# GpSimd makes the second low piece of each half slot of weights, with the residual between them

## The reference

```python
def swiglu(h, w_in, w_out):
    a, u = jnp.split(h @ w_in, 2, axis=-1)
    return (jax.nn.silu(a) * u) @ w_out

def post_norm_residual(x, y, gate, res_w, g, b):
    return layer_norm(DN_ALPHA * x + res_w * (1.0 + gate[:, None, :]) * y, g, b)
...
    mod = c_act @ ada_w[i] + ada_b[i]
    sh0, sc0, g0, sh1, sc1, g1, sh2, sc2, g2 = jnp.split(mod, 9, axis=-1)
```

## Time and profile before

| | |
|---|---|
| median of 3 runs | 4571.94 us (4563.4 to 4573.9) |
| the profiled execution | 4562.87 us, its span 4561.1 us |
| TensorE busy | 3806.3 us (83%) |
| VectorE busy | 3120.1 us (68%) |
| ScalarE busy | 1788.1 us (39%) |
| GpSimd busy | 55.1 us (1%) |
| granted TensorE clock, mean | 0.892 |

### The profile page before, as it was taken

The page is one execution under the profiler, slowest core; times in us unless marked ns, Lnnn a source line. Parts: engine busy times, 40 slices in busy tenths (PEclk is TensorE's granted clock), DMA queues, the critical chain, the costliest instruction groups (busy, mean ns, idle before and its releaser), DMA issues. The chain is left out here.

```text
span 4561.1 us, 65970 instructions
## 1 busy us (share of the span) xinstructions
PE 3806.3 (83%) x26030; PEld 3441.1 (75%) x26030; DVE 3120.1 (68%) x6168; ACT 1788.1 (39%) x3446; POOL 55.1 (1%) x32
## 2 busy tenths in 40 slices
PE   5998899987897752699979987725999799999698
PEld 4986698986797652599879975625998699898587
DVE  6776577765655658866676654488666877687655
ACT  2443444443443230344444442312444444444243
POOL 0000000010000000000000000000000000000000
PEclk9999899997798676699999997765999999999799
DMA  7755475752354121155425542210555366486244
GB/s 295 263 228 196 155 267 215 266 210 102 120 185 157 56 78 43 47 186 191 169 102 185 189 159 96 74 56 29 185 191 188 116 231 234 167 300 245 111 153 148
DMA packets 118965, 751.35 MB, mean 165 GB/s; under 512 B 13184, under 2 KB 13216, under 8 KB 43008
## 3 DMA queue, kind: packets, MB, share of 16 engines
q1 hardware_dynamic: 117648, 742.97, 44.6%
q10 hardware_dynamic: 688, 3.11, 0.2%
q0 software_dynamic: 320, 1.05, 0.1%
HBM read 744.98 MB, written 1.05 MB: 164 GB/s over the span
## 5 line engine op out<-in xcount | busy, mean ns | idle before, releaser
L748 DVE TENSOR_TENSOR weights_low<-weight_ring,weights_high 128x512 fp32r<-128x512 f32 x2248 | 1467.1, 697 | 542.6 <-ACT weights_high L735 529.4
L735 ACT ACTIVATE weights_high<-weight_ring 128x512 fp32r<-128x512 f32 x2248 | 1293.4, 625 | 1069.8 <-PE bank L159 977.6
L159 PE MATMUL bank<-h_high,weights_high 128*128 128x256 f32 x4800 | 1372.0, 286 | 86.2 <-DVE weights_low L748 86.2
L159 PE MATMUL bank<-h_low,weights_high 128*128 128x256 f32 x4800 | 1370.7, 286 | 0.0
L159 PE MATMUL bank<-h_high,weights_low 128*128 128x256 f32 x4800 | 1370.2, 285 | 0.0
L159 PEld LDWEIGHTS bank<-h_high,weights_high 128*128 128x128 f32 x4800 | 933.0, 194 | 105.4 <-issue 88.0
L159 PEld LDWEIGHTS bank<-h_low,weights_high 128*128 128x128 f32 x4800 | 933.1, 194 | 14.4
L159 PEld LDWEIGHTS bank<-h_high,weights_low 128*128 128x128 f32 x4800 | 932.5, 194 | 0.0
L159 PE MATMUL acc<-weights_high,hidden_high 128*128 128x512 f32 x1552 | 609.0, 392 | 3.1 <-DVE weights_low L748 3.1
L159 PE MATMUL acc<-weights_low,hidden_high 128*128 128x512 f32 x1552 | 608.4, 392 | 0.0
L159 PE MATMUL acc<-weights_high,hidden_low 128*128 128x512 f32 x1552 | 603.7, 389 | 0.0
(11 more groups left out here) (254 smaller groups left out, 3386.1 us busy)
## 6 DMA issues: line engine op xcount, KB each, us to landing
weight_ring<-stream SPq DMA_DIRECT2D x582, 1024.0 KB, 4.8
h_tok<-slots SPq DMA_DIRECT2D x96, 512.0 KB, 5.7
h_feat<-slots SPq DMA_DIRECT2D x90, 512.0 KB, 5.8
work<-slots SPq DMA_DIRECT2D x30, 512.0 KB, 7.8
mod_sums<-biases SPq DMA_DIRECT2D x8, 1536.0 KB, 8.2
h_feat<-rows SPq DMA_DIRECT2D x8, 512.0 KB, 4.1
work<-biases SPq DMA_DIRECT2D x1, 1536.0 KB, 9.5
x_tok<-x ACTq DMA_DIRECT2D x1, 1024.0 KB, 11.4
```

What stands on the lines that cost most here:

```text
L159: ins = self.nc.tensor.matmul(out, lhs, rhs, start=start, stop=stop)
L735: act.activation(k.w_hi[:, b, q * self.QUARTER:(q + 1) * self.QUARTER], self.raw(g, q), ACT.Copy).then_inc(k.highs_ready, 1)
L748: ins = dve.tensor_tensor(k.w_lo[:, b, w], self.raw(g, q), k.w_hi[:, b, w].bitcast(F32), ALU.subtract)
```

## The change

The low piece q = 1 of every half is now made by GpSimd, and q = 0 by VectorE as before; each tells TensorE by a semaphore of its own, and TensorE waits for both. `SplitWeights` gets a `gpsimd` method, which replaces `Stage.gpsimd` there: for each half the low piece, and behind those of halves 2, 4, 6 and 8 one of the four operations of the residual. The waits inside the residual (for the rows, and between the multiplications and the additions) stay. `ToTokensAndCouples.gpsimd` still calls its parent's method first, which is now the loop over four halves, and then issues the copies.

```diff
--- before.py
+++ after.py
@@ -106,6 +106,7 @@
         self.slot_landed = [ctx.enter_context(nc.semaphore(f"slot_landed{i}")) for i in range(RING)]
         self.highs_ready = ctx.enter_context(nc.semaphore("highs_ready"))
         self.lows_ready = ctx.enter_context(nc.semaphore("lows_ready"))
+        self.lows_by_pool = ctx.enter_context(nc.semaphore("lows_by_pool"))
         self.halves_used = ctx.enter_context(nc.semaphore("halves_used"))
         self.slots_used = ctx.enter_context(nc.semaphore("slots_used"))
         self.couples_made = ctx.enter_context(nc.semaphore("couples_made"))
@@ -202,8 +203,7 @@
         pass
 
     def gpsimd(self, pool):
-        if self.residual is not None:
-            self.residual.run(pool)
+        pass
 
     def sum_step(self, dve, g):
         for slot in self.macs[g]:
@@ -300,16 +300,20 @@
         for i, place in enumerate(self.places):
             sp.dma_start(place, rows[2 * self.number + i]).then_inc(k.rows_landed, 16)
 
-    def run(self, pool):
-        k = self.k
-        pool.wait_ge(k.rows_landed, 32 * (self.number + 1))
-        for t in range(TT):
+    def part(self, pool, i):
+        k, t = self.k, i % TT
+        if i == 0:
+            pool.wait_ge(k.rows_landed, 32 * (self.number + 1))
+        if i < TT:
             ins = pool.tensor_tensor(k.x[:, t, :], k.h_tok[:, t, :], self.places[0], ALU.mult)
-        ins.then_inc(k.pool_step, 1)
-        pool.wait_ge(k.pool_step, k.step("pool"))
-        for t in range(TT):
+        else:
+            if i == TT:
+                pool.wait_ge(k.pool_step, k.step("pool"))
             ins = pool.tensor_tensor(k.x[:, t, :], k.x[:, t, :], self.places[1], ALU.add)
-        ins.then_inc(k.residual_made, 1)
+        if i == TT - 1:
+            ins.then_inc(k.pool_step, 1)
+        elif i == 2 * TT - 1:
+            ins.then_inc(k.residual_made, 1)
 
 
 
@@ -708,6 +712,7 @@
         for g in range(self.n):
             b = (self.base + g) % DEEP
             pe.wait_ge(k.lows_ready, self.base + g + 1)
+            pe.wait_ge(k.lows_by_pool, self.base + g + 1)
             if g % 2 == 1:
                 k.slots_through()
             self.products(pe, g, k.w_hi[:, b, :], k.w_lo[:, b, :])
@@ -737,17 +742,25 @@
             if g >= 2:
                 self.scalar_after(act, g - 2)
 
+    def low(self, eng, g, q, ready):
+        k = self.k
+        b = (self.base + g) % DEEP
+        w = slice(q * self.QUARTER, (q + 1) * self.QUARTER)
+        eng.wait_ge(k.highs_ready, 2 * (self.base + g) + q + 1)
+        eng.tensor_tensor(k.w_lo[:, b, w], self.raw(g, q), k.w_hi[:, b, w].bitcast(F32), ALU.subtract).then_inc(
+            ready, 1)
+
+    def gpsimd(self, pool):
+        for g in range(self.n):
+            self.low(pool, g, 1, self.k.lows_by_pool)
+            if self.residual is not None and g in (2, 4, 6, 8):
+                self.residual.part(pool, g // 2 - 1)
+
     def vector(self, dve):
         k = self.k
         for g in range(self.n + 2):
-            b = (self.base + g) % DEEP
             if g < self.n:
-                for q in range(2):
-                    w = slice(q * self.QUARTER, (q + 1) * self.QUARTER)
-                    dve.wait_ge(k.highs_ready, 2 * (self.base + g) + q + 1)
-                    ins = dve.tensor_tensor(k.w_lo[:, b, w], self.raw(g, q), k.w_hi[:, b, w].bitcast(F32),
-                                            ALU.subtract)
-                ins.then_inc(k.lows_ready, 1)
+                self.low(dve, g, 0, k.lows_ready)
             if g >= 2:
                 self.vector_after(dve, g - 2)
             self.sum_step(dve, g)
```

## The result

| | before | after |
|---|---|---|
| median | 4568.06 us (4563.4 to 4573.9, 4 runs) | 4610.69 us (4605.55 to 4619.61, 4 runs) |
| span of the profiled execution | 4561.1 us | 4603.8 us |
| TensorE busy | 3806.3 us | 3809.5 us |
| VectorE busy | 3120.1 us | 3034.9 us |
| GpSimd busy | 55.1 us | 1595.3 us |

The account below looks back on a forecast made before the run. TensorE was taken as the bound, with the moved VectorE work nearly all off its path. Terms 15.6 + 17 + 6 + 6.4 + 3 - 4.9 - 1.4 = +41.7 us gave 4614 us, range 4580 to 4662.

Parts of the forecast that it names:

- Starts: At the starts of 26 stages, TensorE begins 0.6 us later because GpSimd makes the second low: +15.6 us.
- The wait behind the residual: VectorE's sum waits for a slot held until the residual's last piece: 8.5 us in two feature stages, 3.0 in two feed-forward.
- Half clock: TensorE gets half its clock behind the residual stalls: 2.2 us per 8.5 us stall, 1.0 per 3 us stall, +6.4 us.
- Gained: Seven short TensorE stalls in the first halves of the stages with a Residual go: -4.9 us.
- Projected: In NSA's "projected" stage, copies behind GpSimd's lows come later and half the 2.72 us stall goes: -1.4 us (+3 if late).
- The dense feed-forward stage: Third part's first feed-forward stage, where VectorE is busiest and the shared port is about full: +3 us (0 to 6).
- Steady stretches: In the peer layers the port needs 2.48 of TensorE's 2.81 us per half: 0; added wait at most 34 us.
- GpSimd's price: One 512-wide low piece on GpSimd was taken to cost 1.25 us, between ends of 1.19 and 2.38.
- Rival B: The SBUF port becomes the bound because a GpSimd low takes 1.45 us or more: 4665 us; chance 0.13.
- Rival D: Stalls compound: late slots keep VectorE late at the next sums and half clock returns, +30, 4644 us; chance 0.14.
- Rival C: Not slower: the sums' slots land before TensorE needs half 7, no stalls there, 4569 us; chance 0.08.

Follow-up runs that it names:

- the pieces alone: Kernel before, but GpSimd does the residual in four pieces after the highs of halves 2, 4, 6, 8; VectorE makes both lows: 4583.33 us, ratio 1.0037.
- the lows alone: Kernel before, but GpSimd makes the second low piece in the 21 stages without a Residual; the other five unchanged: 4579.89 us, ratio 1.0031.

## Why the prediction was right, point by point

The forecast was 4614 us, +42; measured 4610.69, +43. The mechanism of the three large terms, the starts, the wait behind the residual and the half clock behind it, is the one that was forecast, and the runs above bear it out. That the totals agree to 1 us is luck: the terms miss by up to 5 us in both directions, and the measured difference is itself known to some 11 us. The terms, by the traces of the two kernels:

- **Starts**, forecast 0.6 x 26 = 15.6. Counted from ScalarE's first high, TensorE's first product is 0.52 to 0.54 later in all 26, 13.8 us (in six stages TensorE's idle time before it changed by another amount, 0.18 to 2.24 us, as the work before it ended earlier or later); taking them back gave 12 us. The size was a little high since I added the whole of VectorE's first low before GpSimd could begin.
- **The wait behind the residual**, forecast 8.5 twice and 3.0 twice. Measured 7.50, 7.68, 2.48 and 2.63: 20.3 for 23. The term that was too long is the landing, 3.2 us (302.44 to 305.65) where I took 4.1.
- **Half clock**, forecast 6.4. Behind the four stalls, in this order, 24, 27, 16 and 17 products ran at half clock (1.2 GHz), in 5.25, 5.93, 3.51 and 3.53 us, where at full clock one starts every 0.12 us: 10.1 us for these 84, so it cost 8.1. I had given the 3 us stalls 1.0 each; they cost 1.6 and 1.5.
- **Gained**: of the seven stalls of 4.9 us four small ones of 0.42 to 0.47 remain, 1.7 us.
- **"Projected"**, forecast -1.4: this term had the wrong sign. The stall of 2.72 us is gone whole; in "the pieces alone" that stage has it again, at 3.11 us, and in "the lows alone" not. But the copies that now stand behind the four lows end later, and with them the stage. GpSimd's drain at the stage's end (line 180, 181 after) ends 0.2 us after the last copy has landed, in both traces, and all engines wait for it there (the rows below). From the stage's first product to the additions of `Compress` it takes 1041.51 - 1020.52 = 20.99 us before and 1075.04 - 1050.53 = 24.51 after, the later start left out: +3.5 us. "+3 if the copies are late" was the nearer end of the forecast.
- **The dense feed-forward stage**, forecast +3: three stalls of 0.47, 0.47 and 0.74 us, 1.7.
- **Steady stretches**, forecast nothing: the peer stages keep 5.62 us for two halves, and the added wait costs 0 of the 34 us that were its upper bound.

13.8 + 20.3 + 8.1 + 1.7 - 4.9 + 3.5 + 1.7 = +44.2 us, against 42.7 between the two spans. The difference of 1.5 us is within what one execution differs from another: the four runs of the changed kernel lie 14 us apart.

The end of "projected", before and after: GpSimd's drains in the stretch (ns: least/median/most, then the first and last start), and TensorE's first product of the next stage:

```profile
L180 POOLq DRAIN  x2: 41/7706/15371, 1019.9 to 1037.0; - x2
...
1037.02 3.21 PE L159 MATMUL bank<-weight_ring,h_feat 128*128 128x48 f32 x27 [0.72 <-POOLq L180]
...
L181 POOLq DRAIN  x2: 41/5382/10722, 1056.5 to 1067.3; - x2
...
1067.26 7.06 PE L160 MATMUL bank<-weight_ring,h_feat 128*128 128x48 f32 x32 [4.14 <-DVEq L181]
...
1075.04 4.29 DVE L1715 TENSOR_TENSOR work<-work 128x120 f32<-128x120 f32 x16
```

Before, the long drain begins at 1019.9 and lasts 15.37 us, to 1035.2; the last part of the copies landed at 1035.01, ahead of the end of TensorE's last product at 1036.30. After, it begins at 1056.5 and lasts 10.72 us, to 1067.2, where the copies had landed at 1066.99 and TensorE had ended at 1063.12; TensorE starts at 1067.26 after 4.14 idle (the row names VectorE's queue; the drain that came last is GpSimd's). Then it runs the next 32 products at half clock, in 7.06 us; before they took 3.77 at full clock. The gap is 3.20 to 4.31 us in each of the six single-low versions in which GpSimd makes lows in this stage, the changed kernel among them, and 0.72 in the four in which it does not, the kernel before among them. How much of the half clock comes with it differs from run to run, so over all ten traces the stage is 1.6 us longer on average rather than 3.5. No run took this wait away alone, and issuing the copies ahead of the lows was not tried.

GpSimd's price was taken as 1.25 us; it is 1.29 when it does not have to wait for VectorE (the rows at 298.79 and 2042.55). The figure of the Trainium skill (GPSIMD Engine Reference, Elementwise - side-by-side cycle accounting), taken in proportion, had given an estimate of 1.12; the measurement is 15% above it, and half of line 307's 2.38 was the better guide. The row of the dense stage, where the port was to be fullest, beside the earlier trace rows:

```profile
4035.00:4115.00 80.00, 79.07 (x552) 73.94 (x551) 77.78 (x90) 34.41 (x65) 41.68 (x28) 1.00 0.81 301
```

VectorE is busy 77.78 of 80 us with 90 operations where it was 69.61 with 122: it does less and is occupied longer. TensorE still gets 79.07. Rival B needed 1.45 us for a GpSimd low and a stage that falls behind; neither came. The length of whole peer stages shows the same: three of the four keep it within 0.6 us (361.38 us before, 361.39 after in the last), and the one that grew, by 2.2, began at half clock in this execution and at full clock before. Rival D, in which the stalls come again at the next sums, didn't either: after 307.72 no stall follows in that stage. Rival C fell with the slot that VectorE awaited for 12.19 us.

## What to carry to other kernels

Work moved to an idle engine is free only if nobody waits for the slower copy of it: here 0.5 us at each of 26 starts was lost and taking half of the lows, 1124 operations, off a covered engine bought nothing. A task that stands behind new work on an in-order queue moves too, as the four copies did: look at what waits for it. When a side task is cut into pieces and spread over a loop, ask what its completion releases: here a DMA queue held back a transfer, an engine with an in-order list waited for that transfer, and the main engine waited for the next thing on that list. Repair such a chain at its ends, by an earlier last piece or a later first consumer; each gave back about half of the loss.

## What was not expected of the hardware

- Beside GpSimd operations of 1.29 us, VectorE's low of 512 columns takes 1.70 for 0.69, and still TensorE's pace does not change; with two such operations in a row its cast of 256 columns takes 1.26 for 0.29. Yet four GpSimd operations lost only 0.65 us in all to VectorE's four turns in between. The exclusion falls mostly on VectorE: over the changed kernel its 1124 lows take some 480 us more than at 0.69 each, and GpSimd's 1124 some 93 us more than at 1.29.
- The four copies that GpSimd issues in "projected" land in 4.2 and 5.6 us (median of each pair) when they come 9.5 us later, in place of 10.3 and 12.2 us when they were issued together with two slots of the ring and two sums' slots; before, VectorE's sum waited 5.03 us for its slot there and TensorE then 2.72. That the shared transfers made the slot late is argued from this order. All the same the copies end later, as told above. The DMA issues after:

```profile
work<-work POOLq DMA_DIRECT2D x2, 256.0 KB, 4.2
...
work<-work POOLq DMA_DIRECT2D x2, 255.0 KB, 5.6
```

- A stall of 2.48 us in full work was followed by 3.4 us in which TensorE was granted half its clock, here inside half 9 of the feed-forward stage (0,1). The stall's length alone does not decide it: behind the 2.72 us of the kernel before the clock is 1.00 throughout. The two stretches, after and before:

```profile
580.00:582.00 2.00, 2.00 (x11) 2.00 (x11) 0.58 (x1) 0.99 (x2) 0.93 (x1) 0.50 1.03 432
...
1033.00:1037.00 4.00, 3.01 (x12) 2.18 (x12) 0.92 (x2) 0.60 (x1) 0.00 (x0) 1.00 0.98 380
```
